# Self-attention on one core: query blocks in the order 1, 7 to 2, 0, the first index products ahead of the slots, and the modulation pieces in the first stages

## The chip, the core and the metric

One core of one Trainium2 chip. The metric is the device time of one execution in microseconds, the median of several runs. VectorE is DVE in the profile, ScalarE ACT, GpSimd POOL, TensorE PE (products) and PEld (weight loads), SyncE SP.

## The reference

Two blocks of a transformer on a sequence of 1024 rows of width 1024, one after the other: the first has self-attention, attention to a memory and a feed-forward layer, the second a recurrent mixer and a gated feed-forward layer. The change touches the self-attention of the first alone. It has two halves of eight heads of 64 dimensions. The first half looks at a window of 128 keys. The second half picks, for each query, the 256 best of the keys at or before it by an index score, and attends to the latents of these:

```python
dots = einsum('bqhd,bsd->bqhs', iqb, ik) * IDX_DIM ** -0.5
score = einsum('bqh,bqhs->bqs', iwb, relu(dots))
score = where(key_pos <= t, score, NEG_INF)
_, idx = top_k(score, 256)
...
logits = einsum('bqhc,bqkc->bhqk', ql, sel) + bias     # sel: latents of rank 128
p = softmax(logits)
o_lat = einsum('bhqk,bqkc->bqhc', p, sel)
```

Queries come in eight blocks of 128. Block n sees (n + 1) x 128 keys. For blocks 0 and 1 that is no more than 256, so nothing is picked there.

## The kernel before

Everything is resident on one core and float32. After the input projections (up to about 289 us) the kernel runs through `A_SLOTS`, a list of slots (n, i) from n = -1 to n = 8 with eight slots in each n, one for each head. All engines walk through the same list; each takes its own part of a slot's work, and semaphores tie them together.

In slot (n, i) stands, for query block n and head i of the second half: logits of the next slot (TensorE, `sparse_logits`, L718, into one of two pairs of PSUM banks, with the pick mask added by a second product), the bias sum and row maximum (VectorE, L1646 and L1649), the exponential (ScalarE, L1243), the reciprocal of the row sum (VectorE, L1662), the scaling (ScalarE, L1235), the transposes (TensorE L738, copied by ScalarE L1250) and the product with the latents (TensorE L747, copied by ScalarE L1258). The last three belong to the one or two slots before.

Around it goes work for later blocks. The window attention of block n + 1: four products (L677) whose scores VectorE adds to the bias (L1608), maximum (L1614), eight exponentials on ScalarE (L1188, slot 4), row sums (L1623), scaling on GpSimd (L2171), transposes (L686) and output (L695). The index scores of block n + 2: a product for each head in one or two parts of up to 512 columns (L703), a rectifying copy (L1217) and a weighted sum on VectorE (L1631, L1634). GpSimd sets the keys after the query to a large negative value (L2166). The picking of block n + 1 on VectorE (`pick`, L1586): 32 rounds of the eight largest (MAX8, L1594) and their replacement (L1596), four rounds in each slot, the first four in slot 7 of the block before; at the end a mask (L1601). Picking runs over all (m + 1) x 128 columns of block m = n + 1.

Also in these slots are 24 modulation pieces (`ada_columns`, L705): a product of a vector pair with 1024 x 256 weights, eight float32 products of 256 columns each. SyncE loads the weights of each piece, one megabyte, into one of two buffers (L435), and stores every three pieces (L438). Before, they stand in slots 0, 2, 4 and 6 of blocks 1 to 6.

What orders the side work: `shared_jobs` (L78) names the jobs of a slot, and `UJ` numbers them. All of them write PSUM bank 7 and nothing else: each job on TensorE waits until the one before it is emptied. This is the core of it:

```python
def shared(job):
    if UJ[job] > 0:
        pe.wait_ge(u_free, UJ[job])
    return PS[:, 7, :]
```

Ahead of the slots, ScalarE issues the loads of the bias rows (L1180, L1183) and VectorE subtracts a far bias from them (L1637). TensorE waits for these loads (L663) before the first slot. After the slots, ScalarE splits the first block of output weights (L1263, L1093 in the helper), and the next stage begins.

Of the kernel before, what the change touches and what calls it, by code (L numbers as in the profile page):

```python
# [15 lines left out]
P = 128  # L16
# [5 lines left out]
DH = 64  # L22
# [50 lines left out]

A_SLOTS = [(n, i) for n in range(-1, NT + 1) for i in range(NH) if NH * n + i <= NH * NT + 2]
PLACES = ("first", "out", "query0", "banded", "ix0", "ix1", "turned", "ada", "query1")


def shared_jobs(n, i):  # L78

    m, k, h, jobs = n + 1, n + 2 + (i + 1) // NH, (i + 1) % NH, {}  # L80
    if i == 2 and n >= 1:
        jobs["first"] = ("d_out", n - 1)
    if i == 7 and m < NT:
        jobs["out"] = ("a_out", m, 0)
    if i < 3 and 0 <= n < NT:
        jobs["out"] = ("a_out", n, i + 1)
    if m < NT and i < 4:
        jobs["banded"] = ("a_log", m, i)
    if m < NT and i >= 6:
# [9 lines left out]
    if m < NT and i == 6:  # L99
        jobs["query0"], jobs["query1"] = ("query", m, 0), ("query", m, 1)  # L100
    return jobs
# [10 lines left out]
def build_program(nc, I, out):  # L112
    with ExitStack() as ctx:
# [444 lines left out]
        def _(pe):  # L558
# [102 lines left out]
            pe.wait_ge(f_free, FT["memT"])  # L661
            pe.wait_ge(t_free, TT["wo"])
# [9 lines left out]
            def window_logits(m, e):  # L672
                o, lo, q = shared(("a_log", m, e)), max(m - 1, 0), slice(m * P, m * P + P)
                width, r = (m + 1 - lo) * P, e % 2
                hp = slice(DH * r, DH * r + DH)
                for c in (2 * (e // 2), 2 * (e // 2) + 1):
                    ins = pe.matmul(o[:, (c % 2) * 256 + 256 - width:(c % 2) * 256 + 256], lhsT=Q[hp, c, q],  # L677
                                    rhs=kaT[hp, c // 2, lo * P:m * P + P], start=True, stop=True)
                ins.then_inc(u_ready, 1)

            def window_transposes(m, b):
                o = shared(("a_t", m, b))
                pe.wait_ge(s("a_r"), 2 * m + 1 + b // 2)
                for j in range(4):
                    if m > 0 or j % 2 == 1:
                        ins = pe.transpose(o[:, j * P:j * P + P], SB[:, 2 * b + j // 2, (j % 2) * P:(j % 2) * P + P], ident[:, :])  # L686
                ins.then_inc(u_ready, 1)

            def window_out(m, b):
                o = shared(("a_out", m, b))  # L690
                pe.wait_ge(u_free, UJ[("a_t", m, b)] + 1)
                for h in (2 * b, 2 * b + 1):
                    kts = (1,) if m == 0 else (0, 1)
                    for kt in kts:
                        ins = pe.matmul(o[DH * (h % 2):DH * (h % 2) + DH, 0:P],  # L695
                                        lhsT=misc[:, max(m - 1, 0) + kt - (m == 0), DH * (h // 4):DH * (h // 4) + DH],
                                        rhs=PS_T[:, b % 2, 2 * (h % 2) + kt, :], start=(kt == kts[0]), stop=(kt == 1))
                ins.then_inc(u_ready, 1)

            def index_dots(k, h, c):  # L700
                o, hp = shared(("ix", k, h, c)), slice(DH * (h % 2), DH * (h % 2) + DH)
                a, z = BW * c, min((k + 1) * P, BW * c + BW)
                pe.matmul(o[:, 0:z - a], lhsT=iqT[hp, h // 2, k * P:k * P + P], rhs=ikT[hp, a:z], start=True, stop=True).then_inc(u_ready, 1)  # L703
# [8 lines left out]
            def latent_query(n, r):  # L712
                o, q, hp = shared(("query", n, r)), slice(n * P, n * P + P), slice(DH * r, DH * r + DH)
                for j in range(4):
                    ins = pe.matmul(o[:, j * P:j * P + P], lhsT=wukT[hp, j, :], rhs=Q[hp, 4 + j, q], start=True, stop=True)
                ins.then_inc(u_ready, 1)

            def sparse_logits(g):  # L718
                n = g // NH
                pe.wait_ge(u_free, UJ[("query", n, 1)] + 1)  # L720
                if g >= 2:
                    pe.wait_ge(s("d_e"), g - 1)
                if n >= 2:
                    pe.wait_ge(s("picked"), n - 1)
                for a in range(0, (n + 1) * P, BW):
                    z = min((n + 1) * P, a + BW)
                    o = PS[:, 2 * (g % 2) + a // BW, 0:z - a]
                    ins = pe.matmul(o, lhsT=QL[:, g % NH, :], rhs=cT[:, a:z], start=True, stop=(n < 2))  # L728
                    if n >= 2:
                        ins = pe.matmul(o, lhsT=ident_h[:, :], rhs=MSK[:, n % 2, a:z], start=False, stop=True)  # L730
                ins.then_inc(s("d_l"), 1)

            def sparse_transposes(g):
                pe.wait_ge(s("d_n"), g + 1)
                if g >= 1:
                    pe.wait_ge(s("d_te"), g)
                for kt in range(g // NH + 1):
                    ins = pe.transpose(PS[:, 4 + kt // 4, (kt % 4) * P:(kt % 4) * P + P], LG[:, g % 2, kt * P:kt * P + P], ident[:, :])  # L738
                ins.then_inc(s("d_t"), 1)

            def sparse_values(g):
                n = g // NH
# [327 lines left out]
        def _(act):  # L1070
# [113 lines left out]
            def window_exp(m):  # L1184
                w0 = P if m == 0 else 0
# [6 lines left out]
            def empty_shared(job):  # L1192
# [3 lines left out]
                if kind == "a_t":  # L1196
                    m, b = job[1:]
                    if m == 0:
# [3 lines left out]
                elif kind == "a_out":  # L1202
                    m, b = job[1:]
# [4 lines left out]
                elif kind == "d_out":  # L1208
                    n = job[1]
                    ins = act.activation(Q[:, 4:8, n * P:n * P + P], o.rearrange("p (a b) -> p a b", a=4), ACT.Copy)  # L1210
                elif kind == "ix":
                    k, h, c = job[1:]
                    a, z = BW * c, min((k + 1) * P, BW * c + BW)
                    i = NH * (k - 2) + h
# [9 lines left out]

            for n, i in A_SLOTS:
# [6 lines left out]
                if 0 <= g - 1 < NH * NT:  # L1232
                    h, L = (g - 1) % NH, ((g - 1) // NH + 1) * P
# [4 lines left out]
                if 0 <= g < NH * NT:  # L1238
                    L = (n + 1) * P
# [5 lines left out]
                if 0 <= g - 1 < NH * NT:  # L1245
                    h, L = (g - 1) % NH, ((g - 1) // NH + 1) * P
# [14 lines left out]
                if i == 4 and n + 1 < NT:  # L1261
                    window_exp(n + 1)
# [220 lines left out]
        def _(dve):  # L1483
# [98 lines left out]
            dve.wait_ge(s("attn_in"), 16 * 7)  # L1582
# [3 lines left out]
            def pick(m, first, last):  # L1586

                w = (m + 1) * P
                for i in range(first, last):
                    if i == 0:  # L1590
                        dve.wait_ge(s("ix_c"), m - 1)
# [5 lines left out]
                    if i == R8 - 1:  # L1597
                        settled()
                        if m >= 4:
# [4 lines left out]
            def window_scores(m, e):  # L1604
                w0, h0 = P if m == 0 else 0, 4 * (e // 2) + e % 2
# [5 lines left out]
            def window_max(m):  # L1611
                w0 = P if m == 0 else 0
# [14 lines left out]
            def index_sum(k, h):  # L1627
                L, i = (k + 1) * P, NH * (k - 2) + h
                dve.wait_ge(u_free, UJ[("ix", k, h, (L - 1) // BW)] + 1)
                if h == 0:  # L1630
                    dve.tensor_scalar(score[:, 0:L], RL[:, 0, 0:L], iwt[:, k, 0:1], None, ALU.mult).then_inc(s("ix_s"), 1)  # L1631
                else:
                    dve.wait_ge(s("ix_s"), i)
                    dve.scalar_tensor_tensor(score[:, 0:L], RL[:, h % 2, 0:L], iwt[:, k, h:h + 1], score[:, 0:L],  # L1634
                                             ALU.mult, ALU.add).then_inc(s("ix_s"), 1)

            mark(dve.tensor_tensor(bias[:, NH:2 * NH, :], bias[:, NH:2 * NH, :], over_last(far, 2 * P), ALU.subtract))  # L1637
            settled()
            for n, i in A_SLOTS:
                g, m = NH * n + i, n + 1  # L1640
                L = m * P
                if 0 <= g < NH * NT:
                    dve.wait_ge(s("d_l"), g + 1)
                    near = slice(max(n - 1, 0) * P, L)
                    pair = PSf[:, 1024 * (g % 2):1024 * (g % 2) + L]
                    dve.tensor_tensor(pair[:, near], pair[:, near], bias[:, NH + i, (P if n == 0 else 0):], ALU.add).then_inc(s("d_lb"), 1)  # L1646
# [3 lines left out]
                if i < 4 and m < NT:  # L1650
                    window_scores(m, i)
                if n >= 0 and 2 <= n + 2 < NT:
                    index_sum(n + 2, i)
                if i == 4 and m < NT:
# [8 lines left out]
                if 2 <= m < NT and i < 7:  # L1663
                    pick(m, 4 * i + 6, 4 * i + 8)
                if i == 7 and 2 <= n + 2 < NT:
                    pick(n + 2, 2, 4)
                if i == 5 and m < NT:
# [472 lines left out]
        def _(pool):  # L2140
# [20 lines left out]
            offset(0)  # L2161
            for m in range(NT):
                if m >= 2:
                    pool.wait_ge(s("ix_s"), NH * (m - 1))
                    v = score[:, m * P:m * P + P]
                    pool.affine_select(out=v, in_=v, compare_op=ALU.is_ge, fill=NEG, base=0,  # L2166
                                       pattern=[[-1, P]], channel_multiplier=1).then_inc(s("ix_c"), 1)
                w0 = P if m == 0 else 0
# [174 lines left out]
```

## Time and profile before

| | us |
|---|---|
| median of 3 runs | 3803.22 |
| lowest and highest | 3801.25, 3818.11 |
| the profiled execution's own time | 3799.82 |
| its span in the profile | 3798.0 |
| TensorE busy | 3341.8 (88%) |
| VectorE busy | 1476.6 (39%) |
| ScalarE busy | 872.9 (23%) |
| GpSimd busy | 745.3 (20%) |
| mean granted TensorE clock | 0.928 |

The span is the profiled execution from its first to its last instruction; the profile's times count from its start. The attention slots lie between 301.6 and 987 us of it. In rows that give the busy time of stretches, the columns are: the stretch, its length, busy us and number of instructions of PE, PEld, DVE, ACT and POOL, the granted TensorE clock as a share of 2.4 GHz, the busy share of the DMA engines, and GB/s. Rows of groups of instructions give the busy us, the mean ns of one, and the idle time of the engine before them.

### The profile page before, as it was taken

Reading aid. Unit: us, or ns where it says so; the run is one execution under the profiler, and the core shown is the slowest. Engines: PE = TensorE matmul, PEld = TensorE weight load, DVE = VectorE, ACT = ScalarE, POOL = GpSimd, SP = SyncE. Lnnn points to the kernel's source line nnn. Section 1 sums busy time; section 2 is a strip of 40 time slices with the busy share of each in tenths; the row PEclk is TensorE's granted clock in tenths of the full one; section 3 lists DMA queues with packets and bytes.
Section 4 is the critical chain, followed back from the end, with each engine's and each line's share of the span. In section 5 each row is a group of like instructions: output and inputs, shape, how many; then the busy total and the mean of one; then the engine's idle time right before and its main releaser. Section 6 shows DMA issues by size and latency. Waiting matters only on the chain.

```text
span 3798.0 us, 37215 instructions
## 1 busy us (share of the span) xinstructions
PE 3341.8 (88%) x14990; PEld 2463.6 (65%) x14990; DVE 1476.6 (39%) x2594; ACT 872.9 (23%) x1530; POOL 745.3 (20%) x322
## 2 busy tenths in 40 slices
PE   5996888887789878999999977999997589999998
PEld 2443344444677777788888854446877578888886
DVE  3013688998342135322222242302463722222225
ACT  2113333433312212111111122101341122112111
POOL 2000000000321103323323320001111433223223
PEclk9995788888889989999999988999998789999999
DMA  5100111111112101111111131010002202111112
GB/s 143 42 23 22 49 52 45 45 45 23 56 56 95 34 18 43 47 55 44 45 55 44 52 120 53 22 47 0 26 1 97 92 23 56 50 50 44 55 45 111
DMA packets 173178, 192.24 MB, mean 51 GB/s; under 512 B 24268, under 2 KB 137804, under 8 KB 172285
## 3 DMA queue, kind: packets, MB, share of 16 engines
q1 hardware_dynamic: 163696, 177.20, 14.8%
q10 hardware_dynamic: 9356, 13.31, 1.1%
q8 instruction: 87, 1.43, 0.2%
q14 instruction: 39, 0.31, 0.0%
HBM read 174.71 MB, written 15.78 MB: 50 GB/s over the span
## 4 chain that ended last, share of the span: by engine, by line
PE 60%; issue 16%; DVE 13%; POOL 6%; ACT 3%; DMA 1%; ACTq 1%; POOLq 0%; SPq 0%; DVEq 0%
PE psum L606 9%; PE psum L608 9%; PE psum L607 9%; PE psum L599 7%; PE psum L589 6%; POOL weights_parts L2150 3%; PE psum L971 3%; PE psum L709 2%; DVE x_cols L1596 2%; DVE rows L1594 2%; PE psum L703 2%; POOL region L2198 2%; DVE stats L1514 1%; PE psum L747 1%; PE psum L728 1%
## 5 line engine op out<-in xcount | busy, mean ns | idle before, releaser
L2150 POOL TENSOR_TENSOR weights_parts<-weights,weights_parts 128x2048 fp32r<-128x2048 f32 (+1 forms) x82 | 377.0, 4597 | 982.9 <-ACT weights_parts L1093 982.9
L606 PE MATMUL psum<-x_cols_parts,weights_parts 128*128 128x512 f32 x1344 | 525.0, 391 | 25.3 <-POOL weights_parts L2150 23.6
L608 PE MATMUL psum<-x_cols_parts,weights_parts 128*128 128x512 f32 x1344 | 524.3, 390 | 0.0
L608 PE MATMUL psum<-weights_parts,region_parts 128*128 128x512 f32 (+1 forms) x1120 | 410.0, 366 | 0.0
L606 PE MATMUL psum<-weights_parts,region_parts 128*128 128x512 f32 x864 | 337.2, 390 | 6.7 <-DVE region_parts L2104 5.8
L607 PE MATMUL psum<-weights_parts,region_parts 128*128 128x512 f32 x864 | 336.9, 390 | 0.0
L606 PEld LDWEIGHTS psum<-x_cols_parts,weights_parts 128*128 128x128 f32 x1344 | 253.4, 189 | 79.1 <-issue 24.6
L608 PEld LDWEIGHTS psum<-x_cols_parts,weights_parts 128*128 128x128 f32 x1344 | 253.2, 188 | 52.7
L607 PE MATMUL psum<-x_rows_parts,weights_parts 128*128 128x512 f32 x704 | 274.6, 390 | 0.0
L1093 ACT ACTIVATE weights_parts<-weights 128x2048 fp32r<-128x2048 f32 (+1 forms) x82 | 155.0, 1890 | 468.7 <-DMA region<-in_bup_h_dram 142.4
L606 PE MATMUL psum<-weights_parts,x_cols_parts 128*128 128x256 f32 x768 | 222.2, 289 | 27.8 <-POOL wide_parts L2176 11.7
L589 PE MATMUL psum<-x_cols,weights 128*128 128x512 f32 x544 | 234.3, 593 | 1.8 <-ACT x_cols L1126 1.1
L608 PEld LDWEIGHTS psum<-weights_parts,region_parts 128*128 128x128 f32 x1120 | 212.4, 190 | 33.8
L607 PE MATMUL psum<-weights_parts,x_cols_parts 128*128 128x256 f32 x768 | 221.4, 288 | 0.0
L599 PE MATMUL psum<-weights,x_cols 128*128 128x512 f32 (+1 forms) x512 | 200.6, 554 | 0.0
L607 PE MATMUL psum<-wide_parts,weights_parts 128*128 128x512 f32 x512 | 199.9, 390 | 0.0
L606 PEld LDWEIGHTS psum<-weights_parts,region_parts 128*128 128x128 f32 x864 | 162.7, 188 | 41.3 <-DVE region_parts L2104 6.3
L589 PEld LDWEIGHTS psum<-x_cols,weights 128*128 128x128 f32 x544 | 103.1, 190 | 132.4 <-issue 129.5
L2171 POOL TENSOR_TENSOR extra<-extra,rows 128x1024 f32<-128x1024 f32 (+1 forms) x16 | 32.2, 2033 | 788.1 <-DVE rows L1625 788.1
L607 PEld LDWEIGHTS psum<-weights_parts,region_parts 128*128 128x128 f32 x864 | 162.6, 188 | 33.8
L1594 DVE MAX8 rows<-x_cols 128x8 f32<-128x384 f32 (+5 forms) x192 | 171.2, 892 | 6.2 <-POOL x_cols L2166 2.8
L606 PEld LDWEIGHTS psum<-weights_parts,x_cols_parts 128*128 128x128 f32 x768 | 151.8, 198 | 28.9 <-issue 21.6
(285 smaller groups left out, 5185.8 us busy)
## 6 DMA issues: line engine op xcount, KB each, us to landing
weights<-in_ada_w_dram SPq DMA_DIRECT2D x24, 1024.0 KB, 5.2
weights<-in_ffn_up_w_dram SPq DMA_DIRECT2D x44, 512.0 KB, 4.8
weights<-in_w_up_dram SPq DMA_DIRECT2D x16, 1024.0 KB, 5.1
weights<-in_w_down_dram SPq DMA_DIRECT2D x16, 1024.0 KB, 5.1
weights<-in_m_in_w_dram SPq DMA_DIRECT2D x7, 2048.0 KB, 9.1
weights<-in_ffn_down_w_dram SPq DMA_DIRECT2D x10, 1024.0 KB, 5.1
weights<-in_xa_wkv_dram SPq DMA_DIRECT2D x4, 2048.0 KB, 8.0
x_rows<-x_scratch SPq DMA_DIRECT2D x4, 2048.0 KB, 11.3
```

The lines of the kernel that those rows point to most:

```text
L589: m = pe.matmul(o[:, 0:width], lhsT=w[:, k, f * P:f * P + P], rhs=x[:, k, h * width:h * width + width], start=(k == 0), stop=(k == KC - 1))
L599: m = pe.matmul(o[:, 0:z - a], lhsT=x[:, k, t * P:t * P + P], rhs=w[:, k, a:z], start=(k == 0), stop=(k == kc - 1))
L606: pe.matmul(o, lhsT=a_hi, rhs=b_hi, start=(first and i == 0), stop=False)
L607: pe.matmul(o, lhsT=a_hi, rhs=b_lo, start=False, stop=False)
L608: m = pe.matmul(o, lhsT=a_lo, rhs=b_hi, start=False, stop=(last and i == len(terms) - 1))
L703: pe.matmul(o[:, 0:z - a], lhsT=iqT[hp, h // 2, k * P:k * P + P], rhs=ikT[hp, a:z], start=True, stop=True).then_inc(u_ready, 1)
L709: ins = pe.matmul(o[0:2, 0:ADA_W], lhsT=cx[:, k, :], rhs=adaw[:, j % 2, k, :], start=(k == 0), stop=(k == KC - 1))
L971: m = pe.matmul(PS[:, 7, DV * e:DV * e + DV], lhsT=XT[:, k, t * P:t * P + P], rhs=WO_H[b % 2][:, k, :], start=(k == 0), stop=(k == KC - 1))
L1093: act.activation(WHI[buf][:, 0:width], WRAW[buf][:, 0:width], ACT.Copy).then_inc(s("w_hi"), 1)
L1594: mark(dve.max(top, src[:, 0:w]))
L1596: mark(dve.match_replace(work[:, 0:w], top, src[:, 0:w], TAKEN))
L2150: pool.tensor_tensor(WLO[buf][:, 0:width], WRAW[buf][:, 0:width], WHI[buf][:, 0:width], ALU.subtract).then_inc(s("w_lo"), 1)
```

## The change

`ORDER` gives the query block that is worked at each place. Blocks that are picked are those at places 1 to 6. `A_SLOTS` is the same list.

- Order: place 0 works block 1, places 1 to 6 work blocks 7 down to 2, place 7 works block 0. All widths, slices and column ranges follow `ORDER`; the number of a place stays the number in semaphore counts.
- Index scores of the block at place 1 (block 7): TensorE writes its products, two of 512 columns for each head, into the two pairs of logits banks, ahead of the slots and ahead of the wait for the bias rows. ScalarE rectifies 1024 columns at once, VectorE sums all eight heads before it waits for the bias rows and does its subtraction. The other index scores stay in bank 7.
- Picking of the block at place 1: from the first slot of n = -1 on, two rounds in a slot (`FIRST_ROUNDS`), three in each of the last two, 32 in 15 slots. Then as before.
- Modulation pieces: slots 1, 3, 5, 7 of n = -1, all eight slots of n = 0, slots 4 and 5 of n = 1 to 6.
- GpSimd's causal select follows the index sums of each place.

The core of the diff (the rest replaces n, k, m by `ORDER[n]`, `ORDER[k]`, `ORDER[m]` in widths and slices):

```diff
+ORDER = (1, 7, 6, 5, 4, 3, 2, 0)
+FIRST_ROUNDS = (2,) * 13 + (3, 3)
+def picking(n):
+    return 0 <= n < NT and ORDER[n] >= 2
+ADA_SLOTS = [(-1, i) for i in (1, 3, 5, 7)] + [(0, i) for i in range(NH)] + [(n, i) for n in range(1, 7) for i in (4, 5)]
+def pick_rounds(n, i):
+    g = NH * n + i + NH
+    if g < len(FIRST_ROUNDS):
+        a = sum(FIRST_ROUNDS[:g])
+        return 1, a, a + (FIRST_ROUNDS[g] + 1) // 2, a + FIRST_ROUNDS[g]
+    m, r = (n + 2, 0) if i == NH - 1 else (n + 1, 4 * i + 4)
+    return (m, r, r + 2, r + 4) if picking(m) else None
...
-    if k >= 2 and k < NT:
+    if k >= 2 and picking(k):
         jobs["ix0"] = ("ix", k, h, 0)
-        if (k + 1) * P > BW:
+        if (ORDER[k] + 1) * P > BW:
             jobs["ix1"] = ("ix", k, h, 1)
-    if 1 <= n < 7 and i % 2 == 0:
-        jobs["ada"] = ("ada", 4 * (n - 1) + i // 2)
+    if (n, i) in ADA_SLOTS:
+        jobs["ada"] = ("ada", ADA_SLOTS.index((n, i)))
...
             pe.wait_ge(f_free, FT["memT"])
+            b = ORDER[1]
+            for h in range(NH):
+                hp = slice(DH * (h % 2), DH * (h % 2) + DH)
+                if h >= 2:
+                    pe.wait_ge(s("ix0_e"), h - 1)
+                for c in range(2):
+                    m = pe.matmul(PS[:, 2 * (h % 2) + c, 0:(b + 1) * P - BW * c if c else BW], lhsT=iqT[hp, h // 2, b * P:b * P + P],
+                                  rhs=ikT[hp, BW * c:min(BW * c + BW, (b + 1) * P)], start=True, stop=True)
+                m.then_inc(s("ix0_l"), 1)
             pe.wait_ge(t_free, TT["wo"])
             pe.wait_ge(s("attn_in"), 16 * 7)
...
+            L = (ORDER[1] + 1) * P
+            for h in range(NH):
+                act.wait_ge(s("ix0_l"), h + 1)
+                if h >= 2:
+                    act.wait_ge(s("ix_s"), h - 1)
+                act.activation(RL[:, h % 2, 0:L], PSf[:, 1024 * (h % 2):1024 * (h % 2) + L], ACT.Relu,
+                               scale=DH ** -0.5).then_inc(s("ix0_e"), 1)
             for n, i in A_SLOTS:
...
-            dve.wait_ge(s("attn_in"), 16 * 7)
             dve.wait_ge(s("ck_ready"), 2)
...
+            for h in range(NH):
+                index_sum(1, h)
+            dve.wait_ge(s("attn_in"), 16 * 7)
             mark(dve.tensor_tensor(bias[:, NH:2 * NH, :], bias[:, NH:2 * NH, :], over_last(far, 2 * P), ALU.subtract))
...
-                if 2 <= m < NT and i < 7:
-                    pick(m, 4 * i + 4, 4 * i + 6)
-                if i == 7 and 2 <= n + 2 < NT:
-                    pick(n + 2, 0, 2)
+                rounds = pick_rounds(n, i)
+                if rounds:
+                    pick(rounds[0], rounds[1], rounds[2])
                 if 0 <= g < NH * NT:
                     dve.wait_ge(s("d_e"), g + 1)
                     dve.reciprocal(dend[:, i:i + 1], dend[:, i:i + 1]).then_inc(s("d_r"), 1)
...
+            def causal(m):
+                pool.wait_ge(s("ix_s"), NH * m)
+                v = score[:, ORDER[m] * P:ORDER[m] * P + P]
+                pool.affine_select(out=v, in_=v, compare_op=ALU.is_ge, fill=NEG, base=0,
+                                   pattern=[[-1, P]], channel_multiplier=1).then_inc(s("ix_c"), 1)
+            causal(1)
             for m in range(NT):
-                if m >= 2:
+                if m >= 2 and picking(m):
+                    causal(m)
```

## Rows read from the trace of the kernel before

**Rows 1.** The page: the chain that ended last, shares of the span by engine.
```profile
PE 60%; issue 16%; DVE 13%; POOL 6%; ACT 3%; DMA 1%; ACTq 1%; POOLq 0%; SPq 0%; DVEq 0%
```

**Rows 2.** Busy time by stretch, 289 to 987 us (columns as named above).
```profile
289.00:301.60 12.60, 3.58 (x16) 3.18 (x16) 0.01 (x1) 3.67 (x5) 0.00 (x0) 0.50 0.58 167
301.60:321.00 19.40, 10.46 (x38) 8.13 (x40) 5.97 (x11) 4.74 (x20) 2.04 (x2) 0.50 0.00 0
321.00:378.40 57.40, 45.68 (x120) 24.30 (x120) 19.36 (x55) 20.80 (x72) 4.40 (x3) 0.50 0.00 1
378.40:460.80 82.40, 67.72 (x243) 31.57 (x244) 56.74 (x140) 27.83 (x83) 4.49 (x3) 0.73 0.16 52
460.80:544.30 83.50, 67.81 (x285) 32.97 (x284) 67.35 (x140) 32.38 (x89) 4.62 (x3) 0.88 0.16 51
544.30:636.70 92.40, 76.34 (x312) 37.50 (x311) 77.89 (x141) 35.69 (x89) 4.75 (x3) 0.85 0.14 46
636.70:733.50 96.80, 79.62 (x357) 41.85 (x356) 88.23 (x141) 39.08 (x89) 4.88 (x3) 0.89 0.14 44
733.50:839.60 106.10, 86.40 (x404) 48.32 (x403) 98.73 (x140) 42.46 (x89) 5.02 (x3) 0.92 0.12 40
839.60:934.30 94.70, 70.67 (x332) 42.46 (x332) 87.67 (x121) 32.30 (x68) 3.74 (x2) 0.82 0.14 34
934.30:976.50 42.20, 40.10 (x279) 29.77 (x278) 13.80 (x25) 29.99 (x48) 0.00 (x0) 1.00 0.02 1
976.50:987.00 10.50, 7.56 (x70) 6.80 (x69) 0.00 (x0) 4.31 (x8) 0.00 (x0) 1.00 0.01 2
```

**Rows 3.** The chain of waits in 378 to 461 us, by line.
```profile
by line: PE psum L709 27.0%; PE psum L703 12.8%; PE psum L677 6.6%; PE psum L747 5.9%; PE psum L686 5.3%; PE psum L728 5.1%; ACT extra L1188 4.1%; PE psum L715 3.8%; PE psum L695 3.6%; issue 3.4%; DVE x_cols L1596 3.0%; DVE rows L1594 2.6%;
```

**Rows 4.** Groups of instructions by line and form, VectorE, 200 to 1300 us.
```profile
L1594 DVE MAX8 rows<-x_cols 128x8 f32<-128x1024 f32 x32 | 39.2, 1226 | 1.0 <-POOL x_cols L2166 0.5
L1596 DVE MATCH_REPLACE8 x_cols<-rows,x_cols 128x1024 f32<-128x1024 f32 x32 | 38.7, 1208 | 0.0
L1594 DVE MAX8 rows<-x_cols 128x8 f32<-128x384 f32 x32 | 17.9, 558 | 1.0 <-POOL x_cols L2166 0.5
L1596 DVE MATCH_VALUE_LOAD x_cols<-rows,x_cols 128x8 f32 x192 | 17.7, 92 | 6.6
L1634 DVE SCALAR_TENSOR_TENSOR x_cols<-extra,rows,x_cols 128x1024 f32<-128x1024 f32 x7 | 9.5, 1353 | 0.0
```

**Rows 5.** Timeline, 292 to 304 us: start, length, engine, line, operation, idle before.
```profile
292.71 2.19 ACTq L1180 DMA_DIRECT2D x_cols<-bias_scratch  x4
301.59 2.29 DVE L1637 TENSOR_TENSOR x_cols<-x_cols,rows 128x2048 f32<-128x2048 f32 x1 [12.60 <-DMA rows<-bias_scratch]
```

**Rows 6.** The page's group of dense products, and the timeline at 336 to 339 us.
```profile
L589 PE MATMUL psum<-x_cols,weights 128*128 128x512 f32 x544 | 234.3, 593 | 1.8 <-ACT x_cols L1126 1.1
...
336.78 1.64 PE L703 MATMUL psum<-region 64*128 64x384 f32 x2 [0.38 <-DVE extra L1608]
338.46 0.49 ACT L1217 ACTIVATE extra<-psum 128x384 f32<-128x384 f32 x1 [1.75 <-PE psum L703]
```

**Rows 7.** Busy time of two stretches of 10 us.
```profile
370.00:380.00 10.00, 9.16 (x29) 5.44 (x29) 4.99 (x14) 3.16 (x11) 0.00 (x0) 0.50 0.00 0
390.00:400.00 10.00, 8.93 (x36) 3.68 (x35) 3.19 (x8) 2.65 (x8) 0.00 (x0) 0.86 0.31 107
```

**Rows 8.** Three modulation pieces (16 instructions each), by the timeline and the chain.
```profile
389.17 5.38 PE psum L709 x16
...
489.45 6.43 PE L709 MATMUL psum<-weights,cond 128*2 128x256 f32 x16 [0.37 <-ACT extra L1217]
...
645.63 3.62 PE L709 MATMUL psum<-weights,cond 128*2 128x256 f32 x16 [0.69 <-ACT weights L1201]
```

**Rows 9.** Timeline of ScalarE near the end of the attention slots.
```profile
972.03 1.02 ACT L1250 ACTIVATE region<-psum 128x1024 f32<-128x1024 f32 x1 [0.61 <-PE psum L738]
...
986.91 1.90 ACT L1093 ACTIVATE weights_parts<-weights 128x2048 fp32r<-128x2048 f32 x1
```

More of the change, by code:

```diff
@@ L82, in shared_jobs @@
         jobs["first"] = ("d_out", n - 1)
-    if i == 7 and m < NT:
+    if i == 7 and 0 <= m < NT:
         jobs["out"] = ("a_out", m, 0)
@@ L722, in sparse_logits @@
                     pe.wait_ge(s("d_e"), g - 1)
[L723 to L726, printed above, removed]
+                else:
+                    pe.wait_ge(s("ix0_e"), NH - 1 + g)
+                L = (ORDER[n] + 1) * P
+                if picking(n):
+                    pe.wait_ge(s("picked"), n)
+                for a in range(0, L, BW):
+                    z = min(L, a + BW)
                     o = PS[:, 2 * (g % 2) + a // BW, 0:z - a]
-                    ins = pe.matmul(o, lhsT=QL[:, g % NH, :], rhs=cT[:, a:z], start=True, stop=(n < 2))
-                    if n >= 2:
+                    ins = pe.matmul(o, lhsT=QL[:, g % NH, :], rhs=cT[:, a:z], start=True, stop=not picking(n))
+                    if picking(n):
                         ins = pe.matmul(o, lhsT=ident_h[:, :], rhs=MSK[:, n % 2, a:z], start=False, stop=True)
@@ L736, in sparse_transposes @@
                     pe.wait_ge(s("d_te"), g)
-                for kt in range(g // NH + 1):
+                for kt in range(ORDER[g // NH] + 1):
                     ins = pe.transpose(PS[:, 4 + kt // 4, (kt % 4) * P:(kt % 4) * P + P], LG[:, g % 2, kt * P:kt * P + P], ident[:, :])
@@ L1184, in window_exp @@
             def window_exp(m):
-                w0 = P if m == 0 else 0
+                w0 = P if ORDER[m] == 0 else 0
                 act.wait_ge(s("a_m"), m + 1)
@@ L1260, in _ @@
                     job(place)
-                if i == 4 and n + 1 < NT:
+                if i == 4 and 0 <= n + 1 < NT:
                     window_exp(n + 1)
@@ L1611, in window_max @@
             def window_max(m):
-                w0 = P if m == 0 else 0
+                w0 = P if ORDER[m] == 0 else 0
                 dve.wait_ge(u_free, UJ[("a_log", m, 3)] + 1)
@@ L1640, in _ @@
                 g, m = NH * n + i, n + 1
-                L = m * P
                 if 0 <= g < NH * NT:
+                    b = ORDER[n]
+                    L = (b + 1) * P
                     dve.wait_ge(s("d_l"), g + 1)
-                    near = slice(max(n - 1, 0) * P, L)
+                    near = slice(max(b - 1, 0) * P, L)
                     pair = PSf[:, 1024 * (g % 2):1024 * (g % 2) + L]
-                    dve.tensor_tensor(pair[:, near], pair[:, near], bias[:, NH + i, (P if n == 0 else 0):], ALU.add).then_inc(s("d_lb"), 1)
+                    dve.tensor_tensor(pair[:, near], pair[:, near], bias[:, NH + i, (P if b == 0 else 0):], ALU.add).then_inc(s("d_lb"), 1)
                 if 0 <= g < NH * NT:
@@ L1662, in _ @@
                     dve.reciprocal(dend[:, i:i + 1], dend[:, i:i + 1]).then_inc(s("d_r"), 1)
[L1663 to L1667, printed above, removed]
+                if rounds:
+                    pick(rounds[0], rounds[2], rounds[3])
+                if i == 5 and 0 <= m < NT:
                     window_sum(m)
```

79 lines of the change are left out of this document (40 added, 39 removed).

## The prediction

> **What bounds the kernel now.** I read the busy shares first, then a table of stretches cut at the block boundaries of the attention slots, then the chain of waits inside one of them, then the single instructions.
>
> The page says that TensorE products give the kernel its length as a whole: 60% of the chain that ended last [rows 1]. The change touches nothing after the attention slots, so only the stretch from 289 to 987 us counts. There the picture is another one [rows 2]. The first row is the wait ahead of the slots, the second the window work before block 0, then come blocks 0 to 7, and the last row is the tail until the next stage begins. Read the VectorE column against the length. Blocks 4, 5 and 6 have VectorE busy 88 of 97, 99 of 106 and 88 of 95 us: the top-k picking sets their length. Block 0 has it busy 19 of 57 us, block 1 57 of 82, block 7 14 of 42. Those are set by something else. In block 1 the chain of waits names it [rows 3]: the modulation products (L709) are 27% of the chain, 22 us for four pieces, and the index products (L703) 13%; VectorE's picking is 6%. All these products and the window products pass one after the other through PSUM bank 7, each waiting until ScalarE or VectorE has emptied the one before. So VectorE idles about 38 us in block 0, 26 in block 1 and 28 in block 7, and is full in between. What can be gained is idle time of VectorE: 698 us of stretch hold 516 us of its work.
>
> **What the change moves, by stage.** I number the new stages by place: -1 (window work of the first block), 0 (block 1), 1 to 6 (blocks 7, 6, 5, 4, 3, 2) and 7 (block 0). A pick round costs VectorE 1.226 + 1.208 + 0.092 us and a gap of 6.6/192 = 0.03, so 2.56 us at 1024 columns; at 384 the search is 0.558, the replacement about as much, the round 1.23; in between I take 0.27 per 128 columns [rows 4].
>
> Ahead of the slots. Before, TensorE and VectorE both wait until 301.6 for the bias rows that ScalarE asks for at 292.71, and VectorE then spends 2.29 us on a subtraction [rows 5]. After, block 7's eight index products (two of 512 columns each) start at about 293.7, under that DMA wait. That hides 8 us of them and no more. A 512-column float32 product is two instructions of 0.431 us, 0.86 us, in a dense stage at full clock [rows 6], so sixteen take 13.8 us at 2.4 GHz and 27.6 at 1.2. The granted clock in 289 to 301.6 was 0.50 [rows 2]. In 370 to 380 TensorE was 92% busy with 64-row products and transposes and still had 0.50, while in 390 to 400, with an unbroken modulation piece in it, it rose to 0.86 [rows 7]. The new stream is unbroken, but of 64-row products; the two rows point two ways. I take the rise, because only the unbroken stretch resembles it, with the 2 us that a piece caught at the low clock lost against one at full clock (5.38 for 3.62 us) [rows 7, 8]: products end at 293.7 + 13.8 + 2 = 309.5, the last copy (1.2), the last index sum (1.4, L1634 at 1024) and the bias subtraction, which the new code queues behind all eight sums (2.3), give 314.5. With the low clock it is 326. The first window scores and pick rounds queue right behind the subtraction on VectorE, so they start then.
>
> Stage -1. VectorE now has 16 rounds at 1024 columns, 41 us, beside the window work it had (5.97 busy in the old stretch, subtraction included): about 48 us with gaps. Four modulation pieces sit in slots 1, 3, 5, 7. A piece is 3.62 us at full and 6.43 at low clock [rows 8], and about 0.9 more until ScalarE has emptied it, under rounds of 5.1 us a slot: mostly hidden. In the last slot piece, two index products, a window output and a transpose come together, 4.5 + 3.5 + 3 = 11 us against 5. I take 55.
>
> Stage 0. VectorE's load is old block 1's 57 us, plus 9.7 for the rounds (16 of 2.56 and 4 of 2.3 for 28 of 1.23 and 4 of 1.5), plus 2.6 for wider index sums: 69, some 75 with gaps. But this block is bank 7's. Old block 1 took 82.4 us with four pieces and one index product of 512 columns per head. New: four more pieces, 22 us at the chain's price [rows 3]; a second index product of 384 columns for each of eight heads, 1.64 + 0.49 us with their waits about 2.5 at low clock, 1.9 at the old block's 0.73 [rows 6], so 15; no output projection, -2.5. That is 117. The same from old block 0: 57.4, of it 45.7 TensorE at clock 0.50; wider index products add 8 x (0.43 + 1.64) = 16.6 of TensorE at that clock and 7 of waits, eight pieces 51 and 4: 113 of TensorE at the low clock and 23 of other time. At clock 0.75, about the old block 1's, this is 98, at 1.00 79, at 0.50 136. The ends are VectorE's 75 and 136; I take 110, between the two derivations.
>
> Stages 1 to 5 pair with old blocks 5, 4, 3, 2 and 1: the same 28 rounds, but logits two blocks wider (+2.1 us of VectorE), index sums two blocks narrower (-1.9) and the four early rounds two blocks narrower (-2.1). VectorE's load so stays within 2 us. What falls is two of four modulation pieces, which matters where VectorE does not set the length. The pieces in slots 4 and 5 sit beside VectorE's longest slot (the window maximum) but also beside ScalarE's eight window exponentials. Old block 5, 106.1 and full: 105. Old 4, 96.8: 95.5. Old 3, 92.4 with 78 busy: 85. Old 2, 83.5 with 67 busy: 76.5. Old 1, 82.4: two pieces less (-11), no index products and sums and no early rounds (-14), wider logits (+2): 60.
>
> Stage 6, block 2, is old block 0 with no index products (8 of 2.5: -20), with two pieces (+14) and logits of 384 columns for 128: 51. Stage 7, block 0, is old block 7 with each of ScalarE's three wide passes down from 1.02 us to about 0.35 (0.49 was a copy of 384 columns [rows 6]) and smaller products, 2.4 a slot: 42.2 - 19 = 23. The tail's three slots shrink alike: 10.5 to 6 [rows 9]. SP's queue carries the 24 weight loads earlier, two buffers and one megabyte each; they moved 52 GB/s in old block 1 [rows 2], a piece each 20 us; one each 13 us in stage 0 asks for 80 GB/s, less than the 167 GB/s of the first row there. GpSimd's causal select moves with the sums and it waits for nothing later.
>
> Sum: 314.5 + 55 + 110 + 105 + 95.5 + 85 + 76.5 + 60 + 51 + 23 + 6 = 981.5, against 986.91, where ScalarE began the next stage [rows 9]. That is 5.4 us less. The profiled execution took 3799.8 us, 3.4 under the median of 3803.2, so I forecast 3798. The gain is small because the idle time moves: VectorE's 38 + 26 us at the start shrink to some 45 in stages -1 and 0, but stage 6 is a new thin stage, 14 us of VectorE in 51.
>
> **The rivals.** Slower: the new first stages stay at the low clock. Place: the index stream and stage 0. For it speaks 0.50 from 289 to 378 us [rows 2] despite 92% busy in 370 to 380 [rows 7]; against it, that a modulation piece is what raised the clock, and stage 0 has one in every slot. Price: 11.5 us ahead of the slots and, at clock 0.60 in stage 0, 23 + 56.5/0.6 = 117 for the 98 of the second derivation, 19 more, together 30: 3828. It decides once both happen, or once stage 0 lasts over 135 us. Chance 0.15. The Trainium skill, TensorE: Matmul & The Clock Gate, "Why this matters for your kernels", speaks for it: TensorE is to be kept free of idle gaps between bursts of matmuls, or it falls back to its lower clock. By that rule stage 0, whose jobs of bank 7 are parted by copies, would run low and the time be this rival's. The trace agrees in old block 0 and not in old blocks 2 to 6, parted in the same way at 0.82 to 0.92 [rows 2].
>
> Faster: bank 7 is no bound, and VectorE stays fed. Stage 0 then costs 80 to 90 us at a clock near 1.00, stages 3 to 5 come to VectorE's own 82, 71 and 52: 22 + 3 + 5 + 8 less, 38 at the most, 24 likely: 3774. For it speaks the clock of 0.85 and more from old block 2 on; against it the 27% of the chain. Chance 0.25.
>
> A shift without effect: only the index stream runs low and the rest is as forecast: +11.5, 3809. Chance 0.15.
>
> **How the numbers follow.** My forecast has 0.45. About 0.5%, 19 us, is what a measurement of this kernel can tell from no change. The forecast and the third case fall within it; the faster case and the slower one lie beyond. Faster 0.25, same 0.60, slower 0.15. The range takes in the faster case and most of the slower one: 3770 to 3822.
>
> **What would show it.** Right: VectorE's first MAX8 before 330 us, stage 0 clearly longer than its VectorE work, the last two blocks together near 75 us, and the start of the next stage within 10 us of 987. Wrong: stage 0 under 90 us; the index stream's clock; a thin stage 6 over 60 us; pieces that wait for their weights' DMA; any stage from 1 to 4 more than 5 us off.

## The result, and the profile after

The changed kernel takes 3746.9 us in the median (3746.7 to 3752.2) against 3806.5 for the kernel before (now four runs), a ratio of 0.984 with the interval 0.982 to 0.987: 1.6% faster. The forecast was 3798, in a range that began at 3770, so the result lies outside it, on the side of the second rival and well beyond that rival too. The profiled execution fell from 3799.8 to 3746.8 us.

The stretches of the changed kernel, cut where those of [rows 2] are: from VectorE's bias subtraction to its first sum on a block's logits (stage -1), then stages 0 to 7, then the tail. Columns as there.

```profile
311.30:361.30 50.00, 25.52 (x91) 12.11 (x92) 47.40 (x61) 8.50 (x25) 5.95 (x3) 0.68 0.20 63
361.30:469.10 107.80, 87.75 (x309) 35.44 (x309) 71.05 (x105) 32.52 (x90) 4.03 (x3) 0.81 0.24 78
469.10:574.80 105.70, 87.27 (x380) 49.30 (x384) 96.48 (x141) 43.31 (x87) 4.75 (x3) 0.87 0.10 30
574.80:667.20 92.40, 77.08 (x387) 47.06 (x391) 85.93 (x141) 42.74 (x87) 4.62 (x3) 0.93 0.07 23
667.20:747.20 80.00, 65.75 (x334) 41.56 (x335) 75.33 (x140) 36.02 (x78) 4.49 (x3) 0.89 0.08 27
747.20:818.60 71.40, 59.41 (x318) 37.95 (x320) 64.90 (x141) 33.84 (x79) 4.35 (x3) 0.90 0.09 30
818.60:873.50 54.90, 43.40 (x233) 27.18 (x237) 46.89 (x120) 24.84 (x66) 3.75 (x2) 0.88 0.12 39
873.50:913.50 40.00, 33.60 (x226) 22.12 (x225) 11.45 (x35) 23.54 (x71) 2.04 (x2) 1.00 0.14 28
913.50:928.70 15.20, 12.02 (x83) 9.03 (x82) 5.15 (x24) 11.86 (x47) 0.00 (x0) 0.83 0.09 2
928.70:935.10 6.40, 4.26 (x24) 3.04 (x23) 0.16 (x1) 2.21 (x9) 0.00 (x0) 0.50 0.00 0
```

Read the VectorE column (the third of the busy times) against the length, as before. In stages 1 to 5 VectorE is busy 96 of 106, 86 of 92, 75 of 80, 65 of 71 and 47 of 55 us. What it misses there is 5 to 9 us a stage. In stage 0 it is busy 71 of 108 us: that is where it still waits. ScalarE begins the next stage at 935.06, 51.8 us earlier than in [rows 9]; so 51.8 of the 53.0 us lie in the attention stretch.

```profile
935.06 1.90 ACT L1126 ACTIVATE weights_parts<-weights 128x2048 fp32r<-128x2048 f32 x1
```

Ahead of the slots, in the timeline (start, length, engine and line): the index products L688 start at 294.59, under the wait of [rows 5], and the first round of picking at 314.26.

```profile
294.59 3.79 PE L688 MATMUL psum<-region 64*128 64x512 f32 x8 [0.69 <-ACT region L1159]
...
311.33 2.28 DVE L1683 TENSOR_TENSOR x_cols<-x_cols,rows 128x2048 f32<-128x2048 f32 x1
...
314.26 1.22 DVE L1633 MAX8 rows<-x_cols 128x8 f32<-128x1024 f32 x1
```

The granted clock of this stream, in the busy times by stretch (columns as above, the clock is the third number from the end), was 0.56 in its first 4.8 us, then 1.00. The stream is not unbroken: before each pair of heads TensorE waits 0.2 to 1.1 us for ScalarE to empty banks.

```profile
294.60:299.40 4.80, 3.78 (x8) 1.19 (x8) 0.00 (x0) 1.00 (x2) 0.00 (x0) 0.56 0.93 287
299.40:308.60 9.20, 8.69 (x28) 3.91 (x28) 7.17 (x6) 5.74 (x7) 0.00 (x0) 1.00 0.31 79
```

The chain of waits in stage 0 (361 to 469 us), which answers to [rows 3]: the modulation pieces are now L739 and hold 35% of it, the index products L733 21%. And the longest waits of that stretch (engine, line, waited for: us in total, times, longest): VectorE waits 29.9 us for the four window products L707, 13.1 of them at once, at the start of the stage.

```profile
by line: PE psum L739 35.2%; PE psum L733 21.3%; ACT extra L1250 7.4%; PE psum L761 4.9%; PE psum L716 4.4%; PE psum L707 4.2%; ACT extra L1221 3.2%; issue 2.9%; ACT weights L1234 2.8%; DVE extra L1647 2.6%; PE psum L725 2.3%; PE psum L780 
```

```profile
ACT weights L1255 <- PE psum L739: 37.9, 8, 6.2
DVE extra L1647 <- PE psum L707: 29.9, 4, 13.1
ACT extra L1250 <- PE psum L733: 21.3, 18, 2.7
```

### The profile page after: what moved, and what is told of

The parts are those of the page before. It is cut to its first block, busy times and chain, and to the rows that moved or that the text cites. A ratio compares the mean times of both kernels' runs of the same rounds, so it can differ in the third digit from the quotient of the medians.

```text
span 3745.0 us, 37179 instructions
## 1 busy us (share of the span) xinstructions
PE 3297.0 (88%) x14969; PEld 2449.8 (65%) x14990; DVE 1474.7 (39%) x2594; ACT 869.4 (23%) x1522; POOL 745.6 (20%) x322
## 3 DMA queue, kind: packets, MB, share of 16 engines
q1 hardware_dynamic: 163696, 177.20, 15.1%
## 4 chain that ended last, share of the span: by engine, by line
PE 60%; issue 16%; DVE 12%; POOL 6%; ACT 3%; DMA 1%; ACTq 1%; POOLq 0%; SPq 0%; DVEq 0%
PE psum L626 9%; PE psum L628 9%; PE psum L627 9%; PE psum L619 7%; PE psum L609 6%; POOL weights_parts L2194 3%; PE psum L1004 3%; PE psum L739 2%; DVE x_cols L1635 2%; DVE rows L1633 2%; POOL region L2246 2%; DVE stats L1554 1%; PE psum L780 1%; PE psum L733 1%; PE psum L863 1%
## 5 line engine op out<-in xcount | busy, mean ns | idle before, releaser
L1633 DVE MAX8 rows<-x_cols 128x8 f32<-128x1024 f32 (+5 forms) x192 | 171.2, 892 | 5.5 <-POOL x_cols L2209 2.4
L1635 DVE MATCH_REPLACE8 x_cols<-rows,x_cols 128x1024 f32<-128x1024 f32 (+5 forms) x192 | 168.0, 875 | 0.0
```

The source lines that it names most:

```text
L1633: mark(dve.max(top, src[:, 0:w]))
L1635: mark(dve.match_replace(work[:, 0:w], top, src[:, 0:w], TAKEN))
```

## The experiments

All are judged by the median and its ratio, and by the lengths of the stages in one profiled execution each. The rest of the kernel differs by up to 9 us between executions of kernels that share it word for word (from the end of the attention stretch to the end of the span: 2810 us in the changed kernel, 2819 in one of the runs below), so a few us are read from the stage lengths alone. "The stretch" is the time from the bias subtraction to the start of the next stage: 685.3 us before, 623.8 after. The index stream stands ahead of it and is not in it; the subtraction started 9.7 us later than before (311.3 for 301.6), so 61.5 us of the stretch are a net 51.8.

**The order alone.** The pieces go back to their old slots.

```diff
-ADA_SLOTS = [(-1, i) for i in (1, 3, 5, 7)] + [(0, i) for i in range(NH)] + [(n, i) for n in range(1, 7) for i in (4, 5)]
+ADA_SLOTS = [(n, i) for n in range(1, 7) for i in (0, 2, 4, 6)]
```

> The changed kernel with the modulation pieces back in slots 0, 2, 4 and 6 of places 1 to 6; the order stays. Theory A (order and piece slots each do part: with two pieces fewer the middle stages fall to VectorE's own work, the eight pieces in stage 0 cost it some 33 us of bank 7): stage 0 falls from 107.8 to about 75, stages 2 to 5 rise by 4, 10, 9 and 20, stage 6 by 12, time about 3770. Theory B (the order alone does it, the pieces fit anywhere): 3747 within 6.

3755.2 us, ratio 0.988 (0.986 to 0.991), the stretch 634.3. Three quarters of the gain by the ratios, four fifths by the start of the next stage (41.4 of 51.8 us earlier), stay without the new piece slots. Theory B would have had all of it; the time is still nearer to its 3747 than to the 3770 of theory A. Stages 0, 3, 4 and 6, from this kernel's busy times by stretch (columns as in [rows 2]):

```profile
359.50:445.40 85.90, 71.27 (x183) 33.52 (x182) 70.38 (x105) 30.17 (x83) 4.89 (x3) 0.58 0.00 1
...
645.80:732.00 86.20, 74.46 (x369) 44.60 (x372) 75.53 (x141) 37.24 (x79) 4.49 (x3) 0.90 0.16 50
732.00:811.20 79.20, 67.61 (x349) 39.76 (x354) 65.08 (x140) 35.26 (x81) 4.35 (x3) 0.91 0.17 54
...
871.80:924.20 52.40, 45.07 (x256) 27.64 (x255) 11.45 (x36) 24.51 (x73) 2.04 (x2) 0.90 0.17 54
```

Stage 0 is 22 us shorter without its eight pieces (2.7 each), not 33; stages 2 to 6 are longer by 1.8, 6.2, 7.8, 5.7 and 12.4. Expected were 4, 10, 9, 20 and 12: right in stages 4 and 6, too much in 2, 3 and above all 5. Stage 0 was the surprise, with a clock of 0.58.

**The piece slots alone**, in the kernel before, with the order 0 to 7.

```diff
-    if 1 <= n < 7 and i % 2 == 0:
-        jobs["ada"] = ("ada", 4 * (n - 1) + i // 2)
+    if (n, i) in ADA_SLOTS:
+        jobs["ada"] = ("ada", ADA_SLOTS.index((n, i)))
```

> The kernel before with the modulation pieces in the new slots (four in stage -1, eight in stage 0, slots 4 and 5 of 1 to 6); the order stays 0 to 7. Theory A: the pieces lengthen the first two stages, where no picking hides them (19.4 to 45, 57.4 to 95), and save 10, 7 and 6 us in blocks 1 to 3: about 3846. Theory B' (the piece slots are the gain, the order does little): 3806 - 40 = 3766.

3828.3 us, ratio 1.007 (1.005 to 1.009). The new slots alone are a loss, as expected in kind and some six tenths of the 40 us in size: stage -1 takes 27.5 instead of 19.4 us and block 0 84.9 instead of 57.4, where no picking lies beside them. Blocks 1, 2 and 3 gain 12.8, 4.0 and 2.0, but blocks 4 and 5 lose 2.6 and 4.2.

**What the pieces cost.** In the changed kernel, and then in the kernel before, each piece is cut to its first product. This leaves out seven eighths of the modulation products.

```diff
-                for k in range(KC):
-                    ins = pe.matmul(o[0:2, 0:ADA_W], lhsT=cx[:, k, :], rhs=adaw[:, j % 2, k, :], start=(k == 0), stop=(k == KC - 1))
+                for k in range(1):
+                    ins = pe.matmul(o[0:2, 0:ADA_W], lhsT=cx[:, k, :], rhs=adaw[:, j % 2, k, :], start=True, stop=True)
```

> The changed kernel with each modulation piece cut to the first of its eight products, so the modulation vectors are wrong: the price of the pieces where they now stand. Theory A: stage 0 falls from 107.8 to about 75, stage 6 from 40 to about 32, the stages between do not move by more than 1 each: about 3703. Rival (the pieces lie beside picking everywhere): above 3735.

3734.1 us, ratio 0.982 (0.980 to 0.984). That is at the edge of the rival's 3735 and far from the 3703 of theory A: stage 0 falls only to 101.7 us, not to 75. The busy times by stretch of the changed kernel with short pieces, stages 0, 3, 4 and 6:

```profile
358.00:459.70 101.70, 83.39 (x196) 35.50 (x196) 70.47 (x104) 32.61 (x91) 4.88 (x3) 0.53 0.26 83
...
653.10:732.70 79.60, 60.37 (x307) 38.96 (x310) 75.31 (x140) 36.41 (x78) 4.48 (x3) 0.87 0.08 27
732.70:803.40 70.70, 55.48 (x285) 36.35 (x287) 64.91 (x141) 33.88 (x79) 4.35 (x3) 0.86 0.10 31
...
857.20:894.10 36.90, 30.50 (x202) 21.51 (x201) 11.47 (x36) 23.66 (x71) 2.04 (x2) 0.91 0.18 30
```

The granted clock of stage 0 is 0.53 where the full pieces had 0.81, and the products between them are slower for it. The pieces alone (busy us of PE and PEld, clock and DMA as before) keep TensorE busy for 37.9 us of stage 0 in the changed kernel and 8.7 here:

```profile
361.30:469.10 107.80, 37.89 (x132) 12.14 (x133) 0.81 0.24 78
...
358.00:459.70 101.70, 8.69 (x18) 0.78 (x18) 0.53 0.26 83
```

All other work of TensorE there rises from 49.9 (87.75 less 37.89) to 74.7 us (83.39 less 8.69), by 1.50; the clock fell by 1.53. In the timelines of the two kernels (start, length, engine and line) a short piece takes 1.01 us in this one, a full piece 5.18 in the changed kernel:

```profile
377.28 1.01 PE L739 MATMUL psum<-weights,cond 128*2 128x256 f32 x2 [0.69 <-ACT weights L1234]
```

```profile
367.29 5.18 PE L739 MATMUL psum<-weights,cond 128*2 128x256 f32 x16 [0.69 <-ACT weights L1234]
```

So the length of a piece is nearly paid for in stage 0 by the clock that its neighbours have beside it: 29 us less of pieces, 25 us more of the rest. In stages 3 and 4 the two full pieces cost 0.4 and 0.7 us, in stages 1, 2 and 5 3.0, 1.7 and 1.1, in stage 6 3.1. These are the prices of the length, clock included; a short piece still has its place in the queue.

> The kernel before with each modulation piece cut to the first of its eight products, so the modulation vectors are wrong: the price of the pieces where they stood. Theory A: blocks 1, 2 and 3 fall to VectorE's own work, by 20, 10 and 8, blocks 4 to 6 by 5 together: about 3763. Rival (the whole 86 us that the chain of waits gives the pieces over all slots come off): 3720.

3782.2 us, ratio 0.994 (0.993 to 0.996), a gain of about half of what theory A said. Block 3 falls by 11.4 us, block 1 by 7.8, block 2 rises by 2.1. Blocks 1 and 2 have lost clock (0.50 for 0.73, 0.63 for 0.88). The 86 us that the chain gives the pieces, summed over all blocks, are no price: the stretch falls from 685.3 to 660.6 us, by 25.

**Which order.** The same kernel with the narrowest picked block first and the widest last but one.

```diff
-ORDER = (1, 7, 6, 5, 4, 3, 2, 0)
+ORDER = (1, 2, 3, 4, 5, 6, 7, 0)
```

> The changed kernel with the order 1, 2, 3, 4, 5, 6, 7, 0: the first block still picked from stage -1 on, but the narrowest instead of the widest. Theory A (the gain of the order is that the widest picking fills the two stages whose length TensorE sets, and that the widest block is not worked without picking beside it): stages -1 and 0 fall only to about 30 and 95, the block 7 stage without picks takes 60 instead of 40, time about 3758. Rival (only the narrow last block matters): 3747.

3818.5 us, ratio 1.003 (1.002 to 1.005): the whole gain is gone, and 60 us more than expected. The stretch is 689.1 us. Its busy times by stretch, stages -1, 0, 6 and 7:

```profile
305.40:341.90 36.50, 24.44 (x84) 11.12 (x86) 26.19 (x61) 8.22 (x24) 5.95 (x3) 0.73 0.26 87
341.90:433.70 91.80, 77.28 (x290) 32.70 (x290) 42.13 (x104) 27.65 (x81) 4.48 (x3) 0.80 0.28 92
...
908.90:968.60 59.70, 54.02 (x343) 36.89 (x345) 16.80 (x35) 35.65 (x70) 2.04 (x2) 0.99 0.12 19
968.60:989.40 20.80, 16.97 (x126) 13.84 (x124) 5.20 (x25) 13.57 (x48) 0.00 (x0) 0.94 0.01 2
```

Stages -1 and 0 are 29 us shorter, but VectorE does 50 us less in them (68 for 118), and stages 1 to 7 take 96 us more. VectorE's own work there is 55 us of the 96 (441 for 386); the rest is more idle time, 14 of it in stage 6, where the widest block now comes with no picking beside it and takes 59.7 us for 40.0, as expected. What theory A missed are stages 1 to 5. So a narrow last block and picking from stage -1 on are not enough. The run turns the whole order round, and so does not part what the widest picking at the start gains from what the widest block near the end costs.

**The wait for the bias rows.** The index products are issued after it.

```diff
+            pe.wait_ge(t_free, TT["wo"])
+            pe.wait_ge(s("attn_in"), 16 * 7)
+            pe.wait_ge(s("cx_ready"), 1)
             b = ORDER[1]
             for h in range(NH):
...
-            pe.wait_ge(t_free, TT["wo"])
-            pe.wait_ge(s("attn_in"), 16 * 7)
-            pe.wait_ge(s("cx_ready"), 1)
```

> The changed kernel with the index products ahead of the slots issued after TensorE's wait for the bias rows instead of before it. Theory A: the first pick starts 8 us later (322 instead of 314) and nothing absorbs it: 3755. Rival (stage 0's slack absorbs it): 3747.

3759.2 us, ratio 0.987 (0.984 to 0.989). The subtraction starts at 320.1 instead of 311.3, 8.7 us later. The wait itself is 8.3 of it: the products start 12.7 us behind the transposes L678 instead of 4.4. The stream took 1.8 us longer, at a clock of 0.72 for 0.85, and all this started 1.4 us sooner. The stretch behind it is 624.4 us, the same. Nothing absorbs the wait: as expected.

**Bank 7.** The first twelve pieces go to bank 5, with semaphores of their own.

```diff
-                o = shared(("ada", j))
+                if 0 < j < N_OWN:
+                    pe.wait_ge(s("ada_f"), j)
+                o = PS[:, 5, :] if j < N_OWN else shared(("ada", j))
```

> The changed kernel, its first twelve modulation pieces (stages -1 and 0) written to PSUM bank 5, which is idle in those stages, with semaphores of their own; nothing else moves. Theory A (stage 0 is bound by bank 7, whose users wait for each other's copies): each of the eight pieces of stage 0 loses the wait before it and the copy after it, about 1.5 us, and its window scores come sooner: stage 0 falls from 107.8 to about 95, time about 3734. Rival (TensorE in program order, not the bank, is the limit): stage 0 within 4 of 107.8, time 3743 to 3750.

3743.1 us, ratio 0.983 (0.980 to 0.985), not to be told from the changed kernel by the median. By the stages: 48.3 and 100.3 us for -1 and 0, 9 less than the 157.8 after. Stage 0 lies between the 95 of theory A and the rival's 104: the bank costs a bit under 1 us a piece, not 1.5. That TensorE's own program order holds the rest is argued, not tried.

**The rounds of the first block.** One in each of the first eight slots, the others in stage 0.

```diff
-FIRST_ROUNDS = (2,) * 13 + (3, 3)
+FIRST_ROUNDS = (1,) * 8 + (4, 4, 4, 3, 3, 3, 3)
```

> The changed kernel with the first block's picking moved from stage -1 to stage 0: one round in each of the first eight slots, then 4, 4, 4, 3, 3, 3, 3. Theory A (stage -1 is bound by VectorE's rounds, stage 0 is not, with 37 us of VectorE idle): stage -1 falls from 50 to about 30, stage 0 rises by at most 5, time about 3731. Rival (the rounds of stage 0 lie on its path too): stage 0 rises by the 20 us that stage -1 loses, 3747.

3748.2 us, ratio 0.984 (0.981 to 0.986). Stages -1 and 0 take 36.4 and 116.1 us, 5 less together. Stage 0 rises by 8, stage -1 falls by 14, neither theory A's 5 for 20 nor the rival's 20 for 20. The fourth piece of stage -1 ends 50 us behind the subtraction instead of 61, in both kernels 11 to 13 us into stage 0, and VectorE's longest wait for window products L707 is 15.1 for 13.1 us. This fits two stages that are one queue of TensorE, in which a split of VectorE's work moves little; it is not shown by itself. The profiled execution lost 5 us ahead of the stretch, where the index stream ran at a clock of 0.52 (below).

> The changed kernel with the first twelve pieces in bank 5 and the first block's rounds moved to stage 0 (one in each of the first eight slots, then 4, 4, 4, 3, 3, 3, 3). Theory A (after the rounds move, stages -1 and 0 are bound by TensorE's jobs in their order alone, 152.5 us together; bank 5 shortens that): 145 us together, 3737. Rival (VectorE's rounds in stage 0 now bind): 150 or more, 3745.

Both together: 3739.9 us, ratio 0.983 (0.981 to 0.985), 33.1 and 110.6 us, 143.7 for the two stages. The two gains, 9 and 5, add up to the 14, as theory A said.

**A better version.** The pieces are spread to where VectorE is full, four instead of eight in stage 0.

```diff
-ADA_SLOTS = [(-1, i) for i in (1, 3, 5, 7)] + [(0, i) for i in range(NH)] + [(n, i) for n in range(1, 7) for i in (4, 5)]
+ADA_AT = {-1: (1, 3, 4, 5), 0: (2, 3, 4, 5), 1: (2, 3, 4, 5), 2: (2, 3, 4, 5), 3: (3, 4, 5), 4: (4, 5), 5: (4, 5), 6: (4,)}
+ADA_SLOTS = [(n, i) for n in range(-1, 7) for i in ADA_AT[n]]
```

> The changed kernel with the pieces spread by the idle time of TensorE beside picking: 4 in stage -1 (slots 1, 3, 4, 5), 4 in stage 0 (2 to 5), 4 each in stages 1 and 2 (2 to 5), 3 in stage 3, 2 each in 4 and 5, 1 in 6. Theory A (a piece costs 2.7 us in stage 0, 3 in stage 6 and 0 to 1 beside a pick that fills VectorE): stages -1 and 0 together fall from 158 to about 140, stages 1 to 3 rise by 3 together, stage 6 falls by 3: about 3729. Rival (with fewer pieces stage 0 loses its clock, as it did with short pieces): stages -1 and 0 within 6 of 158, 3744.

3733.5 us, ratio 0.982 (0.980 to 0.983), between theory A's 3729 and the rival's 3744. The stretch is 610.6 us, 13 shorter than in the changed kernel, though the intervals of the two ratios overlap. Its busy times by stretch, stages -1, 0, 1 and 2:

```profile
308.30:359.80 51.50, 32.08 (x107) 14.06 (x108) 47.37 (x61) 8.87 (x26) 5.95 (x3) 0.67 0.25 82
359.80:452.40 92.60, 75.89 (x245) 33.41 (x245) 70.43 (x104) 31.42 (x87) 4.88 (x3) 0.76 0.15 46
452.40:554.60 102.20, 89.39 (x394) 49.12 (x399) 96.59 (x141) 43.23 (x86) 4.75 (x3) 0.87 0.13 42
554.60:647.30 92.70, 82.32 (x418) 47.84 (x423) 86.06 (x141) 43.62 (x89) 4.62 (x3) 0.94 0.14 46
```

Stage 0 falls by 15 us at a clock of 0.76, and stages 1 and 2 carry four pieces each at no cost. Stage 6, with one piece for two, did not fall (41.4); its clock is 0.82 for 1.00.

> The same spread, and its first eight pieces in PSUM bank 5. Theory A: what bank 5 gave before (7.4 us for eight pieces in stage 0) comes for four, 3 to 4 us more: about 3726. Rival (the slots without pieces were the ones that gained): equal to the spread alone within 1.

3736.4 us, ratio 0.980 (0.978 to 0.983), the stretch 610.6 us again: stages -1 and 0 are 1.9 us shorter, stage 1 1.7 longer. Equal, as the rival said.

## Why the prediction was wrong

**What bounds the kernel**: right, and it held. VectorE's idle time was the thing to gain. It was 170 us of the 685 before (516 busy) and is 119 of 624 after. The forecast named this and then gave most of it back. It also called VectorE "full in between", which [rows 2] do not bear out: it was idle for 16 us in block 2 and 14.5 in block 3.

**Ahead of the slots**: 314.5 said, 314.3 measured, in part by luck. The clock did rise in the stream, and the end terms were about right. But other kernels that share this code up to the subtraction had other clocks in it. These are the changed kernel, the rounds moved late, and the spread pieces, each from the first to the last of the sixteen products:

```profile
294.59:308.57 13.98, 12.48 (x36) 5.11 (x36) 7.17 (x6) 6.70 (x7) 0.00 (x0) 0.85 0.52 150
...
292.87:311.80 18.93, 17.44 (x35) 7.07 (x36) 7.17 (x6) 6.26 (x7) 0.00 (x0) 0.52 0.39 111
...
293.10:305.52 12.42, 10.68 (x36) 4.61 (x36) 7.18 (x6) 6.69 (x7) 0.00 (x0) 1.00 0.58 169
```

So the third case on record, a stream at the low clock, did come in an execution of the same code. From the first product to the subtraction it cost 22.1 us for 16.7, 5.4 more and not 11.5.

**Stage 0**: 110 said, 107.8 measured, with the clock at 0.81. Bank 7 was taken for its bound; moving the pieces out of it took off 7.5 us, no more. The number was right by its two derivations; its terms were not. I priced a piece at 5.5 us from the chain of waits. Without any piece the stage takes 85.9, so eight cost 2.7 each, 22 us for my 44, and the rest of my sum was 66 for 86, since a stage without pieces has the low clock (0.58). That the two errors cancel is luck. That the chain's share is no price is shown in both kernels by the short pieces.

**Stages 1 to 5** were the first step that failed. I wrote that VectorE's load stays within 2 us of the paired old block, which is nearly so: 2.2 to 2.6 less (96.5 for 98.7, 85.9 for 88.2, 75.3 for 77.9, 64.9 for 67.4). Then I kept most of the old blocks' waits: 105, 95.5, 85, 76.5 and 60 against 105.7, 92.4, 80.0, 71.4 and 54.9 measured, 17.6 too much. The two pieces of slots 4 and 5 cost 0.4 to 3 us a stage there, while four in slots 0, 2, 4 and 6 cost up to 7.8 more (order alone). "Where VectorE does not set the length" was read from the old blocks; in the new stages 1 to 5 VectorE is idle for no more than 9.2 us each, so it does set it there too. Nearly half of the fall in stages 2 to 4 is not the pieces. With the pieces in their old slots these stages take 94.2, 86.2 and 79.2 us, 2.6, 6.2 and 4.3 under the old blocks that they pair with. The forecast put the fall on the pieces alone. VectorE's smaller load is some 2.4 of it in each; that the rest is the narrower index products is argued, not tried.

**Stage -1**: 55 from the first round said, 47.0 measured (314.3 to 361.3). I put the backlog of the last slot into this stage. It came in stage 0, whose first slot holds the 13.1 us wait; together the two stages were 10 too long.

**Stages 6 and 7 and the tail**: 51, 23 and 6 said, 40.0, 15.2 and 6.4 measured, 18.4 too much: the second failed step. Stage 6 was priced from old block 0, whose 45.7 us of TensorE ran at a clock of 0.50 [rows 2], with +14 for its two pieces. It ran at 1.00. Short pieces gave 36.9 us at 0.91, so the length of the two pieces cost 3.1, and that term was 11 too large, the whole error. The rest of the sum, 37, hit the 36.9 in part by chance, as it was worked out at the other clock. How much of the 11 us is the clock was not tried by itself; the run with the late stream, the same code here, had 0.92 and took 42.6. In stage 7 I took 2.4 us off a slot of 4.8. Four of its slots take 1.2 to 1.6. VectorE's row maximum shrinks with the block too, 1.22 us over 1024 columns and 0.29 over 128, and the sum left it out. From VectorE's bias sum to the next one, in the timeline:

```profile
921.94 0.28 DVE L1693 TENSOR_TENSOR psum<-psum,x_cols 128x128 f32<-128x128 f32 x1
922.26 0.29 DVE L1696 TENSOR_REDUCE rows<-psum 128x1 f32<-128x128 f32 x1
...
923.08 0.16 DVE L1708 RECIPROCAL rows<-rows 128x1 f32<-128x1 f32 x1 [0.53 <-ACT region L1283]
...
923.15 0.28 DVE L1693 TENSOR_TENSOR psum<-psum,x_cols 128x128 f32<-128x128 f32 x1
```

The errors sum to the difference: 8 in stage -1, 2 in stage 0, 18 in 1 to 5, 18 in 6, 7 and the tail, 46 us.

**The signs.** The first MAX8 before 330 us came (314.3), and so did a stage 0 longer than VectorE's work (107.8 for 71.1). The last two blocks took 55 us, not 75, and the next stage began 52 us before 987. Of the signs of being wrong one came, and barely: stage 4 was 5.1 us off.

**The rivals.** The slower one failed on its place: the index stream had 0.56 rising to 1.00, stage -1 0.68 and stage 0 0.81. Its mechanism showed where pieces are missing: stage 0 fell to 0.58 and 0.53. The Trainium skill (TensorE: Matmul & The Clock Gate, "Why this matters for your kernels") wants TensorE free of idle gaps between bursts of matmuls. The traces do not bear out that gaps made this difference: in stage 0 TensorE's longest gap was 4.3 us in the changed kernel, at 0.81, and 3.7 with short pieces, at 0.53, and all others were at most 0.8 us in both. The faster one had the right sign and in part the wrong reason: bank 7 holds 9 us of the first two stages, and stage 0 was 108, not 80 to 90. What it said of stages 3 to 5, VectorE's own 82, 71 and 52, came true within 3 us.

## What to carry to other kernels

When one engine's work grows over a triangular loop, try the widest block first if its work can lie beside a stretch that another engine bounds, and the narrow ones last: here the order alone gave 1.2%, and the ascending order none. Price a moved job by the stage it lands in, with the stage's own bound and clock, and not by its share in the chain of waits. When a stage is paired with an old one, ask for each wait of the old one whether its cause is still there; waits and prices copied from old blocks were some 29 of the 46 us of this error (stages 1 to 6).

## What was not expected of the hardware

A stage of short dependent products ran at a granted clock of 0.53 to 0.58 without long pieces and at 0.81 with one in each slot; shortening the pieces from 16 instructions to 2 took only 6 of its 108 us off. And TensorE, busy 92% with 64-row products and transposes in [rows 7], stayed at 0.50. The stream of 64-row products, with the same code ahead of and in it, was at 1.00 throughout in one execution, rose to 1.00 in the changed kernel, and stayed at 0.52 in another, with TensorE busy for 17.4 of its 18.9 us. A forecast that hangs on such a rise is a forecast of chance.
